# A block of expert gathers: three picks gathered in halves into spent rows, and the weighted residual made on GpSimd

## What is computed

```python
hn = rmsnorm(h, ln_ffn_w[l])
q = (hb @ w_q).reshape(n, PEER_HEADS, 2, PEER_HALF)
s = jnp.einsum('nhid,hikd->nhik', q, sub_keys)
s_top, i_top = lax.top_k(s, PEER_TOPK)
cand = s_top[:, :, 0, :, None] + s_top[:, :, 1, None, :]
...
best, pos = lax.top_k(cand.reshape(n, PEER_HEADS, PEER_TOPK * PEER_TOPK), PEER_TOPK)
w = jax.nn.softmax(best, axis=-1)
u = jnp.take(u_tab, idx, axis=0)
act = jax.nn.gelu(jnp.einsum('nhkd,nd->nhk', u, hb))
out = jnp.einsum('nhk,nhkd->nd', w * act, jnp.take(v_tab, idx, axis=0))
```

## Time and profile before

| what | value |
|---|---|
| time, median of 3 runs | 1489.49 us (1488.85 to 1489.63) |
| the profiled execution | 1489.38 us, span 1487.5 us |
| TensorE matmul busy | 1358.6 us (91%) |
| VectorE busy | 1063.6 us (71%) |
| ScalarE busy | 679.0 us (46%) |
| GpSimd busy | 299.7 us (20%) |
| gathers' queue (q0) | 268.45 MB, 43.5% of 16 DMA engines' span |
| all other loads (q1) | 149.17 MB, 30.9% |

### The profile page before, as it was taken

How to read it: one execution, slowest core, us unless ns; L and a number is a source line. 1 busy time by engine, 2 the same in 40 slices (tenths; PEclk the granted TensorE clock), 3 DMA queues, 4 the chain that set the end, 5 groups by cost and what they waited for, 6 DMA issues and landing times.

```text
span 1487.5 us, 18142 instructions
## 1 busy us (share of the span) xinstructions
PE 1358.6 (91%) x6729; PEld 979.7 (66%) x6729; DVE 1063.6 (71%) x2114; ACT 679.0 (46%) x1246; POOL 299.7 (20%) x260
## 2 busy tenths in 40 slices
PE   9999999999999887877778887788999999999998
PEld 9999989789895333333323333333499888998876
DVE  6977688766698776777777677665787665766664
ACT  7765976575553222222122222222364575645673
POOL 0000000000035544544535443542200000000000
PEclk9999999999999999898999898999999999999999
DMA  8554555455979999999999999999765555554542
GB/s 303 157 171 142 185 176 168 143 167 178 340 285 394 421 421 422 421 421 422 421 421 420 422 421 422 421 421 422 311 233 172 168 184 184 162 178 143 164 147 85
DMA packets 78487, 418.78 MB, mean 282 GB/s; under 512 B 8816, under 2 KB 9008, under 8 KB 45376
## 3 DMA queue, kind: packets, MB, share of 16 engines
q0 software_dynamic: 36864, 268.45, 43.5%
q1 hardware_dynamic: 41536, 149.17, 30.9%
HBM read 416.51 MB, written 1.08 MB: 281 GB/s over the span
## 4 chain that ended last, share of the span: by engine, by line
PE 57%; DMA 28%; DVE 8%; ACT 2%; issue 2%; POOL 2%; DVEq 0%; POOLq 0%; ACTq 0%
PE ps L1118 15%; DMA AR<-in_peer_uv,C 15%; PE ps L1120 14%; PE ps L1119 14%; DMA SLAB<-in_peer_uv,C 14%; PE ps L1435 6%; DVE AR L2371 1%; DVE wlo L2072 1%; DVE SLAB L2371 1%; POOL SLAB L2624 1%; POOL AR L2624 1%; ACT whi L1613 1%; PE ps L1368 1%; ACT AR L1832 0%; PE ps L1352 0%
## 5 line engine op out<-in xcount | busy, mean ns | idle before, releaser
L2072 DVE TENSOR_TENSOR wlo<-raw,whi 128x1024 fp32r<-128x1024 f32 x246 | 298.8, 1221 | 148.9 <-ACT whi L1613 148.6
L1613 ACT ACTIVATE whi<-raw 128x1024 fp32r<-128x1024 f32 x246 | 259.0, 1056 | 119.6 <-PE ps L1120 104.0
L1435 PE MATMUL ps<-SLAB,AR 128*128 128x512 f32 x520 | 255.0, 641 | 59.1 <-ACT AR L1832 59.1
L1435 PE MATMUL ps<-AR 128*128 128x512 f32 x504 | 249.3, 645 | 59.0 <-ACT AR L1832 58.9
L2624 POOL DMA_INDIRECT AR<-in_peer_uv,C x126 | 146.9, 1166 | 594.3 <-DVE C L2028 418.0
L1118 PE MATMUL ps<-XH,whi 128*128 128x256 f32 (+1 forms) x896 | 260.6, 291 | 0.6 <-DVE XL L2312 0.6
L1120 PE MATMUL ps<-XH,wlo 128*128 128x256 f32 (+1 forms) x896 | 254.2, 284 | 0.0
L1119 PE MATMUL ps<-XL,whi 128*128 128x256 f32 (+1 forms) x896 | 254.1, 284 | 0.0
L1435 PEld LDWEIGHTS ps<-SLAB,AR 128*128 128x128 f32 x520 | 104.3, 205 | 205.5 <-issue 124.1
L1435 PEld LDWEIGHTS ps<-AR 128*128 128x128 f32 x504 | 101.2, 205 | 200.2 <-issue 116.9
L2371 DVE CUSTOM_DVE_ANT_0 SLAB<-SLAB,AR 128x1024 f32<-128x1024 f32 x130 | 158.3, 1224 | 73.2 <-DMA SLAB<-in_peer_uv,C 73.2
(11 more groups left out here) (406 smaller groups left out, 1718.7 us busy)
## 6 DMA issues: line engine op xcount, KB each, us to landing
raw<-in_stream SPq DMA_DIRECT2D x246, 512.0 KB, 3.9
AR<-in_stream SPq DMA_DIRECT2D x9, 512.0 KB, 7.0
AR<-scr SPq DMA_DIRECT2D x8, 512.0 KB, 5.2
SLAB<-in_peer_uv,C POOLq DMA_INDIRECT x130, 28.0
AR<-in_rows SPq DMA_DIRECT2D x4, 512.0 KB, 5.1
AR<-in_peer_uv,C POOLq DMA_INDIRECT x126, 28.0
AR<-in_con SPq DMA_DIRECT2D x1, 1280.0 KB, 6.2
AR<-in_xin SPq DMA_DIRECT2D x2, 512.0 KB, 9.7
```

The costliest lines, as they stand in the source:

```text
L1435: t = pe.matmul(ps[2 * i + half][:, :], d, rows_in[:, 512 * half:512 * half + 512], start=c == 0, stop=c == 127)
L1613: a.activation(in_two(whi[i % NS][:, :]), src, ACT.Copy).then_inc(*hi.up(i))
L2072: v.tensor_tensor(in_two(wlo[i % NS][:, :]), src, in_two(whi[i % NS][:, :]).bitcast(F32), ALU.subtract).then_inc(*lo.up(i))
```

## The change

Three more picks may be held early, in slots numbered 17, 18 and 19 (`HALVES`). Such a slot has no space of its own. It is made of the u halves of two other slots (1 and 2; 7 and 8; 3 and 4), which are spent when the dots of the two picks in them are done. The pick's u goes into one, its v into the other, by two indirect DMAs of 4 KB rows; VectorE computes the two row numbers (2 * index and 2 * index + 1) in the step `gather`. Each is used at most once, for a pick below 32, and is preferred over other free slots. The two lenders are not gathered into again before the `sum` of the pick in the borrowed halves. `rows_weighted` is said much earlier, right after `h_root` (during projection tile 113), and made by GpSimd; ScalarE's squares are dumped elsewhere.

```diff
@@ -99,6 +99,7 @@
 FIRST_PQ = LAST["out"] + 1
 
 EARLY, TILES, SLOTS = 9, 10, 17
+HALVES = {SLOTS: (1, 2), SLOTS + 1: (7, 8), SLOTS + 2: (3, 4)}
 SPARE_OF = (7, 7, 6, 4, 4, 5, 5, None, 0, 0, None)
 EXTRA = [FIRST_PQ + NR + n for n in range(len(SPARE_OF))]
 IN_RING = [i for i in range(len(KINDS)) if i not in EXTRA]
@@ -540,6 +541,7 @@
     def second_half():
         yield from h_turned(1)
         yield say("h_root")
+        yield say("rows_weighted")
 
     mid.append(second_half())
 
@@ -575,6 +577,11 @@
     holds, slot_of = {}, {}
 
     def slot_free(j):
+        if j in HALVES:
+            return j not in holds and all(p in holds and ("dot", holds[p]) in done for p in HALVES[j])
+        for e, lenders in HALVES.items():
+            if j in lenders and e in holds and ("expert", holds[e]) not in done:
+                return False
         if j in holds:
             return ("expert", holds[j]) in done
         if j < EARLY:
@@ -587,10 +594,13 @@
 
     def gather(m):
         names = [j for j in range(SLOTS if m < LAST_WIDE else TILES) if slot_free(j)]
+        if m < 32:
+            names += [j for j in HALVES if slot_free(j)]
         if not names:
             return None
-        j = min(names, key=lambda j: holds.get(j, -1))
-        before = holds.get(j)
+        j = min(names, key=lambda j: (j not in HALVES, holds.get(j, -1)))
+        before = max([holds[p] for p in HALVES[j]] if j in HALVES else
+                     [holds[e] for e in (j, *HALVES) if e in holds and (e == j or j in HALVES[e])], default=None)
         slot_of[m], holds[j] = j, m
         return say("gather", m, j, before)
 
@@ -618,7 +628,6 @@
 
         yield from gathers(8)
         yield from first_topk.go()
-        yield say("rows_weighted")
         yield from gathers()
         for _ in range(4):
             yield PAUSE
@@ -1012,6 +1021,7 @@
         SUBK = place("SUBK", 6144, 2048)
         HN = place("HN", 0, 2048).rearrange("p (i d) -> p i d", i=2)
         QT = place("QT", 13824, 1024).rearrange("p (b f t) -> p b f t", b=2, f=2)
+        spent = [place("spent", c, 1024).rearrange("p (i c) -> p i c", i=2) for c in (8192, 13824)]
         S = [place(f"S{i}", 8192 + 2048 * i, 2048).rearrange("p (f k) -> p f k", f=16) for i in range(2)]
         TV = place("TV", 12288, 32).rearrange("p (s k) -> p s k", s=2)
         TI = place("TI", 12320, 32).rearrange("p (s k) -> p s k", s=2)
@@ -1032,12 +1042,20 @@
         slots += [SUBK]
         slots += [SLAB[:, 2048 * j:2048 * j + 2048] for j in range(NS)]
         slots += [SLAB[:, 2 * NS * CH + XW * j:2 * NS * CH + XW * j + 2048] for j in range(2)]
+        first_halves = lambda pair, c: pair.rearrange("p (a c) -> p a c", a=2)[:, :, c:c + 1024]
+        slots += [first_halves(AR[:, 14848:18944], 0), first_halves(SLAB[:, 2 * NS * CH:2 * NS * CH + 2 * XW], high),
+                  first_halves(AR[:, 18944:23040], 0)]
+
+        def row_half(j, n):
+            return slots[j][:, n, :] if j in HALVES else slots[j][:, 1024 * n:1024 * n + 1024]
+
         spare = [(SLAB, 2 * NS * CH + high), (SLAB, 2 * NS * CH + high + CH), (AR, 3072), (AR, 20992), (AR, 22016), (AR, 23040), (AR, 24064),
                  None, (AR, 4096), (AR, 5120), None]
         in_two = lambda ap: ap.rearrange("p (a c) -> p a c", a=2)
         late_scores = in_two(place("S", 8192, 4096))
         extra = {i: in_two(home[0][:, home[1]:home[1] + CH]) for i, home in zip(EXTRA, spare) if home}
         extra[EXTRA[7]], extra[EXTRA[10]] = late_scores[:, :, 1024:1536], late_scores[:, :, 1536:2048]
+        HALF_ROWS = SM[:, 500:506].bitcast(U32).rearrange("p (e n) -> p e n", e=3)
         iota16 = C1[:, C_IOTA:C_IOTA + 16]
         gfin = place("gfin", 9216, 1024)
         J = place("J", 10240, 512)
@@ -1102,7 +1120,7 @@
-        s_uv = [sem(f"expert_rows{j}") for j in range(SLOTS)]
+        s_uv = [sem(f"expert_rows{j}") for j in range(SLOTS + len(HALVES))]
@@ -1421,11 +1439,11 @@
                 elif step == "gather":
                     m, j, _ = at
                     slot_of[m], uses[j] = j, uses.get(j, 0) + 1
-                    summed[m] = (s_uv[j], 16 * uses[j])
+                    summed[m] = (s_uv[j], 32 if j in HALVES else 16 * uses[j])
                 elif step == "sum":
                     m, group = at
                     i, c = pick_of(m)
-                    d, rows_in = DG[:, m % 4, :], slots[slot_of[m]][:, 1024:2048]
+                    d, rows_in = DG[:, m % 4, :], row_half(slot_of[m], 1)
                     h, k = divmod(c, 16)
                     on.wait_ge(*(dve.of(("diagonal", m)) if group is None else act.of(("diagonal", m))))
                     on.wait_ge(*summed[m])
@@ -1780,7 +1798,7 @@
                     blk, tt, i, b = at
                     if blk == 0:
                         on.wait_ge(*dve.of(("out_add", 0, tt)))
-                        a.activation(HN[:, tt, 0:512], H[:, tt, 0:512], ACT.Square, accum_out=SM[:, 24 + tt:25 + tt]).then_inc(*act.up())
+                        a.activation(spent[0][:, tt, :], H[:, tt, 0:512], ACT.Square, accum_out=SM[:, 24 + tt:25 + tt]).then_inc(*act.up())
                 elif step == "h_turn":
                     k, = at
                     on.wait_ge(*side.of(("h_turn", k)))
@@ -1790,7 +1808,7 @@
                 elif step == "h_root":
                     for i in range(2):
                         on.wait_ge(*dve.of(("out_add", 1, i)))
-                        a.activation(HN[:, i, 512:1024], H[:, i, 512:1024], ACT.Square,
+                        a.activation(spent[1][:, i, :], H[:, i, 512:1024], ACT.Square,
                                      accum_out=SM[:, 26 + i:27 + i]).then_inc(*act.up("h_squares"))
                     root("h", SM[:, 24:26])
 
@@ -2354,19 +2372,21 @@
                         v.reciprocal(SM[:, 29:30], SM[:, 29:30]).then_inc(*dve.up())
                         on.wait_ge(*dve.now())
                         v.tensor_scalar(w, w, SM[:, 29:30], None, ALU.mult).then_inc(*dve.up(("weights", n)))
-                elif step == "rows_weighted":
-                    on.wait_ge(s_rows, GAINS["ffn"])
-                    for i in range(2):
-                        v.tensor_tensor(HN[:, i, :], H[:, i, :], GW, ALU.mult).then_inc(*dve.up("rows_weighted"))
                 elif step == "gather":
                     m, j, _ = at
+                    if j in HALVES:
+                        i, c = pick_of(m)
+                        on.wait_ge(*dve.of("first_picks" if m < 8 else ("picks", m // 16)))
+                        for n in range(2):
+                            v.tensor_scalar(HALF_ROWS[:, j - SLOTS, n:n + 1], IDX[:, i, c:c + 1], 2.0, float(n), ALU.mult, ALU.add).then_inc(
+                                *dve.up(("half_rows", j)))
                     slot_of[m], uses[j] = j, uses.get(j, 0) + 1
-                    landed[m] = (s_uv[j], 16 * uses[j])
+                    landed[m] = (s_uv[j], 32 if j in HALVES else 16 * uses[j])
                 elif step == "dot":
                     m, = at
                     i, c = pick_of(m)
-                    u = slots[slot_of[m]][:, 0:1024]
-                    on.wait_ge(*dve.of("rows_weighted"))
+                    u = row_half(slot_of[m], 0)
+                    on.wait_ge(*pool.of("rows_weighted"))
                     on.wait_ge(*landed[m])
                     v.tensor_tensor_reduce(u, u, HN[:, i, :], 1.0, 0.0, ALU.mult, ALU.add, AV[:, i, c:c + 1]).then_inc(*dve.up(("dot", m)))
                 elif step == "weigh":
@@ -2603,14 +2623,21 @@
             on = Passed(g)
             uses = {}
             for step, *at in order_of_work():
-                if step == "gather":
+                if step == "rows_weighted":
+                    on.wait_ge(s_rows, GAINS["ffn"])
+                    on.wait_ge(*dve.of(("out_add", 1, 1)))
+                    for i in range(2):
+                        g.tensor_tensor(HN[:, i, :], H[:, i, :], GW, ALU.mult).then_inc(*pool.up("rows_weighted"))
+                elif step == "gather":
                     m, j, before = at
                     i, c = pick_of(m)
                     on.wait_ge(*(dve.of("first_picks") if m < 8 else dve.of(("picks", m // 16))))
-                    if before is not None:
+                    if j in HALVES:
+                        on.wait_ge(*dve.of(("dot", before)))
+                    elif before is not None:
                         on.wait_ge(*side.of(("sum", before)))
                     elif j < EARLY:
-                        on.wait_ge(*(dve.of("rows_weighted") if j == 6 else dve.of(("root", "h"))))
+                        on.wait_ge(*(pool.of("rows_weighted") if j == 6 else dve.of(("root", "h"))))
                         on.wait_ge(*prod.of((LAST["out"], 1)))
                         if j in SPARE_OF:
                             on.wait_ge(*lo.of(max(e for e, of in zip(EXTRA, SPARE_OF) if of == j)))
@@ -2621,7 +2648,13 @@
                     else:
```

(8 more changed lines are left out.)

## The result

The changed kernel takes 1497.56 us (median of 5, 1496.13 to 1499.63) against 1489.43 (1488.69 to 1489.63) before: ratio 1.0054, 95% interval 1.0043 to 1.0064. It is slower by 8.1 us, as to the sign what was forecast, but 4.5 us more than the forecast and above the range. The profiled execution has a span of 1495.8 us against 1487.5, +8.3.

The account below looks back on a forecast made before the run. The prediction took the gathers' stage to be bound by DMA bytes at 421 GB/s. It summed 1489.38 + 2.0 (queue) + 1.6 (product) = 1493.0, with the runs' median 0.1 higher: 1493.1 us, range 1489.0 to 1496.8.

Parts of the forecast that it names:

- the queue's: Gather queue, three half picks: a longer dry stretch while gather 10 waits for dot 5; +2.0 us, middle of two prices.
- the product's: Near 403 us: GpSimd's product delays VectorE's `wlo` (0.9 us) and one more two-input operation (0.7 us); +1.6 us.
- The order of the gathers: Start of the gathers: gather 8 fills the hole, gather 10 waits for dot 5, ending at 451.2 us, holding later gathers.
- the hole at 441 us: From 440 to 464 us the kernel before moves 345 GB/s, not 421: 4.3 us lost, the most that filling can give.
- the step by bytes: Queue priced by the mean engine: dry from 446.3 to about 454.0 us, 7.3 us lost against 4.3; +3.0 us.
- the step by landings: Queue priced by the slowest engine: gather 14 lands at 468.3 us instead of 467.2; +1.1 us.
- The price of 4 KB rows: Half picks' transfers: at the weight loads' 378 GB/s, 0.28 us more a pick, 0.84 us for three.
- B: Rival: the product disturbs nothing, the hole in the gather queue stays; some 1491.5 us, chance 0.22.
- C: Rival: the product disturbs nothing, and VectorE's 2.3 us saved reach dot 5 after all; 1489.2 us, chance 0.15.
- D: Rival: the gather queue never runs dry because dot 5 is done in time; 3.5 us gained, 1486.0 us, chance 0.09.
- Case A: The forecast itself: queue's and product's costs both happen; 1493.1 us, own range 1491.5 to 1496.5, chance 0.50.
- case E: Rival: GpSimd's products last over 2 us and hold VectorE twice, with the bytes' price; 1496.4 us or more, chance 0.04.

Follow-up runs that it names:

- two half slots: Kernel before plus two half slots (slots 1 and 2; 3 and 7), taken only when no other is free, product on VectorE: 1486.92 us against 1489.38, ratio 0.9984.
- half slots taken last: Changed kernel with one edit, a half slot is taken only when no other slot is free: 1494.08 us, ratio 1.0031 to the kernel before.
- a third half slot: Third half slot, of slots 8 and 6, added to the kernel before with two, product on VectorE: 1489.25 us against 1489.48 for the kernel before.
- the half picks alone: Changed kernel with the product back on VectorE in its old place, half picks and order of gathers kept: 1494.60 us, ratio 1.0037 to the kernel before.
- the 32 picks measured in a full queue: Kernel before with picks 96 to 127 gathered in two halves into their own slots: 1491.94 us against 1489.38, ratio 1.0020.
- the product alone: Changed kernel without its half picks, the product still early on GpSimd: 1492.57 us against 1489.60 for the kernel before, ratio 1.0018.
- the product added: Kernel before with GpSimd's early product added and VectorE's kept in its old place: 1493.20 us, ratio 1.0024.

## Why the prediction was wrong, and where it was right

Both terms of the sum were too small: the queue's, +2.0 against 4.4 to 5.0 measured, and the product's, +1.6 against 3.0 to 3.8. The order of the gathers and the waits were as predicted.

- **What bounds the stage, and the hole at 441 us:** right. Removing the hole (two half slots) moves the last dot by 3.4 us in the profiled execution, of 4.3 - 0.6 = 3.7 estimated, and the median of the runs by 2.5.
- **The order of the gathers and the wait for dot 5:** right. Gather 8 fills the hole, gather 10 stands at the head of GpSimd's queue, and the saved 2.3 us of VectorE end at the `whi` of the next tile. With half slots taken last one transfer moves before the wait and 2.8 us come back; a third half slot with this wait costs 2.3 us against the kernel without it (1489.25 against 1486.92).
- **The size of the queue's term failed:** predicted +2.0 (1.1 to 3.0), measured +4.4 by bytes and last dot and +5.0 by the runs (the half picks alone). 1.0 of the missing 2.4 us came in when the step by bytes (+3.0) was averaged with the step by landings (+1.1). The step by landings let the engines that lag catch up in the dry time for good: gather 14 did land only 3.2 us later than before (461.4 + 9.0 = 470.4 against 467.2), but at dot 40 the shift is 4.7. Why the lag comes back was not tried. The other 1.4 us are in the step by bytes itself, 8.7 us lost against 7.3: it let the queue run at 421 GB/s from 454.0 us on, where 217 GB/s moved until 456 us and 322 until 458. Two things stand beside this slow filling in the rows. GpSimd starts the first half 0.8 us after its row numbers are made (451.39 to 452.16), where the gathers of before start 0.3 us after their indices. And a pick in halves costs GpSimd about 3.1 us for its two issues, which is 1.049 MB / 3.06 us = 343 GB/s, less than the 421 that the queue can move; the five issues of gathers 10 to 12 take 8.0 us, 2.67 for each pick. Whole gathers filled the empty queue faster, at the start of the stage. That the issues set the pace is read from these rows; no run changed it alone.
- **The price of 4 KB rows:** 0.84 us predicted for three, 0.24 by the 32 picks measured in a full queue.
- **The product on GpSimd:** the mechanism right, the size too small: +1.6 predicted, 3.0 to 3.8 measured in the runs, 3.3 before the first gather in the profile after (3.54 less 0.28 of an earlier shift). The prediction had 0.9 for the `wlo` and 0.7 for what the second product meets. The `wlo` took 2.0: a product lasts 2.34 us where it isn't held itself (4.69 for two), twice what the prediction took. The second product met an operation on two columns (0.76 us instead of 0.16), and what follows stands no more than 2.0 us later, so this part was 0. The other 1.3 are a step that the prediction didn't have: TensorE's idle 2.56 us and its half clock behind it. Three of the four profiles with this idle time show the half clock (the changed kernel, the product alone, the product added, each with a stretch of 2 us at 0.50). In the fourth, with half slots taken last, the `wlo` also took 3.23 us and TensorE also waited 2.56, but the granted clock stayed 1.00 through 407 to 413 us. The first gather came at 421.01 us there, 2.0 later than before once the earlier shift of that profile (0.53) is taken off: the `wlo` alone.
- **The Trainium skill's rule** ("SBUF — State Buffer", section "Who interferes with whom"), that a VectorE instruction with two SBUF inputs is kept out by a GpSimd instruction that reads SBUF and not by one that only writes it: the runs agree, the two-input `wlo` is held 2.0 us beside a GpSimd product and 0.0 beside a memset. The price that the prediction worked out from the Trainium skill ("GPSIMD Engine Reference", section 3.1), an estimated 2.25 us for a product, is near the measured 2.34, and the term of 2.0 that came of it would have been the better one.
- **The rivals:** the product that disturbs nothing (B, C) falls by the product alone and the added product; the queue that never runs dry (D) is what two early half slots do, but not the changed kernel. Case A's two mechanisms happened, the product's term in the upper part of its bounds and the queue's above its bound; the time that came of it is the one of case E (1496.4 or more), which had a chance of 0.04. Its products of over 2 us happened, but of the two times that they held VectorE only the first cost anything.

## What to carry to other kernels

A borrowed buffer is worth what its last condition is worth: order picks by when their wait can be met, for in an engine's strict queue the wait for one late dot held two transfers whose slots had long been free. A half slot that was ready 9 us before the queue ran dry gave 2.7 us; three of them, the second with a condition met 5 us after the queue of that kernel ran dry (446 us), cost 5.0. And work moved to GpSimd isn't free because GpSimd is idle: look at what VectorE and the engines behind it do in those microseconds, the shortest operations too.

## What the runs showed of the hardware

- A GpSimd product (2.34 us for 128x1024) held VectorE operations whose inputs are in SBUF until it ended, however short they are: a `TENSOR_TENSOR` of two columns went from 0.16 to 2.04 us, a `TENSOR_SCALAR`, with a single tile as input, from 0.17 to 2.27. The XL operations with one input in PSUM stayed at 1.65 us for four; a GpSimd memset (two in 1.84 us) held nothing.
- After 2.56 us without a matmul TensorE was at half clock for some 3.4 us in the changed kernel (16 matmuls at a pace of 0.21 us instead of 0.12), and at full clock throughout after the same gap with half slots taken last.
- Gathers of 4 KB rows cost 0.08 us for 1.05 MB more than those of 8 KB (2.6 us for 32), while plain weight loads with such rows run at 378 GB/s.
- Whole gathers filled the empty queue to 418 GB/s from 3.5 us after the first issue on; gathers in halves, 3.1 us of GpSimd's issues for each pick, moved 178, 217 and 322 GB/s in the first 6 us.
